# Two decoder blocks on one core: factors shared by two engines, a mask and a norm in other places of VectorE's order, transposes by halves, and the end of a convolution one chunk sooner

## The reference

```python
h = rms_norm(x, norm_mix)
proj = h @ w_in            # sb q,k,v | gla q,k,v | g_out | g_low | two gates
log_a = log_sigmoid(g_low @ w_gate_up + b_gate_up) / 16
o_gla = gla_chunked(g_q, g_k, g_v, log_a)      # 4 heads, key width 128, value width 256
o_gla = rms_norm(o_gla, gla_norm) * silu(g_out)
mix = sigmoid(gate_sb) * (o_sb @ w_proj_sb) + sigmoid(gate_gla) * (o_gla @ w_proj_gla)
x = x + mix @ w_out
x = x + square(relu(rms_norm(x, norm_mlp) @ w_ff1)) @ w_ff2
x = rms_norm(x, norm_final)
...
xn = rms_norm_2(x, norm_mix_2)
proj = xn @ w_in_2         # nsa q, kv, gates | conv a, ag | mem q | three merge gates
kvm = rms_norm_2(mem, norm_mem) @ w_mem_kv     # its second half is vm
u = a * sigmoid(ag)
u = conv_general_dilated(pad(u), conv_w, 31 taps, depthwise) + conv_b
u = silu(layer_norm(u, conv_ln_g, conv_ln_b))
br_conv = u @ w_conv_out
merged = gm[0] * br_nsa + gm[1] * br_conv + gm[2] * br_mem
h = x + merged @ w_out
out = h + (silu(hn @ w_gate) * (hn @ w_up)) @ w_down    # hn = rms_norm_2(h, norm_ffn)
```

## Time and profile before

| | |
|---|---|
| median of 3 runs | 941.41 us (940.28 to 945.93) |
| profiled execution, its time | 946.68 us |
| profiled execution, its span | 944.9 us |
| mean granted TensorE clock over the span | 0.992 |
| TensorE matmul busy | 918.0 us (97%) |
| VectorE busy | 623.9 us (66%) |
| ScalarE busy | 518.3 us (55%) |
| GpSimd busy | 93.1 us (10%) |

### The profile page before, as it was taken

The page is one execution under the profiler, slowest core; times in us unless marked ns, Lnnn a source line. Parts: engine busy times, 40 slices in busy tenths (PEclk is TensorE's granted clock), DMA queues, the critical chain, the costliest instruction groups (busy, mean ns, idle before and its releaser), DMA issues.

```text
span 944.9 us, 14354 instructions
## 1 busy us (share of the span) xinstructions
PE 918.0 (97%) x5800; PEld 813.2 (86%) x5800; DVE 623.9 (66%) x773; ACT 518.3 (55%) x728; POOL 93.1 (10%) x200
## 2 busy tenths in 40 slices
PE   8998999999999999999999999999998999999998
PEld 7996778899989888888879988889997788888887
DVE  5533565877766655566685888878967576566564
ACT  6544675665546444444466778876354555444451
POOL 8503343231010000000000000000000000000000
PEclk9998999999999999999999999999999999999999
DMA  8654242447555555555564852444435455655551
GB/s 270 201 179 133 92 131 89 135 147 251 173 180 179 174 198 205 181 178 178 181 179 132 266 179 90 135 134 126 138 98 176 133 179 183 205 185 182 178 178 45
DMA packets 115673, 155.36 MB, mean 164 GB/s; under 512 B 2649, under 2 KB 94913, under 8 KB 115618
## 3 DMA queue, kind: packets, MB, share of 16 engines
q1 hardware_dynamic: 114704, 151.57, 49.3%
q0 software_dynamic: 864, 2.98, 0.9%
q10 hardware_dynamic: 50, 0.04, 0.0%
HBM read 153.53 MB, written 1.05 MB: 164 GB/s over the span
## 4 chain that ended last, share of the span: by engine, by line
PE 80%; DVE 7%; ACT 7%; issue 3%; POOL 2%; DMA 1%; SPq 0%; ACTq 0%; DVEq 0%; POOLq 0%
PE PS L604 16%; PE PS L606 16%; PE PS L605 16%; PE PS L929 15%; PE PS L931 8%; DVE wlo L1791 3%; ACT whi L1232 2%; POOL TMP L224 2%; PE PS L831 1%; PE PS L1062 1%; PE PS L1040 1%; ACT TMP L1600 1%; PE PS L974 1%; DMA res<-in_x_dram 1%; DVE hT L1875 1%
## 5 line engine op out<-in xcount | busy, mean ns | idle before, releaser
L1791 DVE TENSOR_TENSOR wlo<-raw,whi 128x2048 fp32r<-128x2048 f32 x140 | 322.1, 2301 | 165.1 <-ACT whi L1232 165.0
L1232 ACT CAST whi<-raw 128x2048 fp32r<-128x2048 f32 x141 | 268.7, 1906 | 124.0 <-PE PS L606 124.0
L929 PE MATMUL PS<-hT,whi 128*128 128x512 f32 x608 | 216.9, 400 | 1.5 <-DVE hT L1875 1.5
L604 PE MATMUL PS<-hT,whi 128*128 128x256 f32 (+1 forms) x616 | 177.1, 288 | 2.3 <-DVE hT L1875 2.1
L605 PE MATMUL PS<-hT,whi 128*128 128x256 f32 (+1 forms) x616 | 174.2, 283 | 0.0
L606 PE MATMUL PS<-hT,wlo 128*128 128x256 f32 (+1 forms) x616 | 174.2, 283 | 0.0
L931 PE MATMUL PS<-hT,wlo 128*128 128x256 f32 x608 | 171.0, 281 | 0.0
L929 PEld LDWEIGHTS PS<-hT,whi 128*128 128x128 f32 x608 | 114.9, 189 | 30.1 <-issue 1.7
L604 PEld LDWEIGHTS PS<-hT,whi 128*128 128x128 f32 (+1 forms) x616 | 117.5, 191 | 4.0 <-issue 2.7
L605 PEld LDWEIGHTS PS<-hT,whi 128*128 128x128 f32 (+1 forms) x616 | 117.5, 191 | 0.2
L606 PEld LDWEIGHTS PS<-hT,wlo 128*128 128x128 f32 (+1 forms) x616 | 117.5, 191 | 0.0
(11 more groups left out here) (360 smaller groups left out, 1287.0 us busy)
## 6 DMA issues: line engine op xcount, KB each, us to landing
raw<-in_w_in_dram SPq DMA_DIRECT2D x47, 1024.0 KB, 5.2
raw<-in_w_ff_dram SPq DMA_DIRECT2D x32, 1024.0 KB, 5.2
raw<-in_w_gate_dram SPq DMA_DIRECT2D x11, 1024.0 KB, 5.3
raw<-in_w_up_dram SPq DMA_DIRECT2D x11, 1024.0 KB, 5.3
raw<-in_w_down_dram SPq DMA_DIRECT2D x11, 1024.0 KB, 5.0
raw<-in_w_out_dram SPq DMA_DIRECT2D x8, 1024.0 KB, 4.9
raw<-in_w_proj_gla_dram SPq DMA_DIRECT2D x4, 1024.0 KB, 5.0
raw<-in_w_mem_kv_dram SPq DMA_DIRECT2D x4, 1024.0 KB, 5.1
```

Source lines behind the costliest of these rows:

```text
L604: pe.matmul(dst, a_hi, b_hi, start=start, stop=False, skip_group_check=True)
L929: pe.matmul(PS[:, bank + c, :], w_hi[:, k, f], hT[:, k, :, :].rearrange("p w t -> p (w t)"), start=k == 0, stop=False, skip_group_check=True)
L1232: act.copy(whi[:, n % RING, :], raw[:, n % RING, :]).then_inc(hi_made, 1)
L1791: dve.tensor_tensor(wlo[:, n % RING, :], raw[:, n % RING, :], whi[:, n % RING, :].bitcast(F32), ALU.subtract).then_inc(lo_made, 1)
```

## The change

Five edits. (1) Units 0 and 1 are shared between GpSimd and VectorE as units 5 to 7 are (`SHARED_UNITS`, `upper_factors`, at chunks 9 and 11). (2) The norm of head 0 moves on VectorE from behind the mask of chunk 14 to a place ahead of the split of chunk 17. (3) At chunk 18 the mask of unit 4 moves on VectorE from behind the split of chunk 21 to a place between the banks of gout2 and gout3; its reduce stays. (4) VectorE scales x in four half pieces, first both first halves, and TensorE turns the first two pairs half a token block sooner in vm1, the other two where it turned all. (5) The last steps of the convolution move from s = 29 to s = 28, VectorE's product ahead of the split and ScalarE's rounding behind it; seven taps move from late and middle places to others.

```diff
-        LATE_UNITS, LOW_LEVELS = (5, 6, 7), 4
+        SHARED_UNITS, LOW_LEVELS = (0, 1, 5, 6, 7), 4
...
-                for l in range(LOW_LEVELS if u in LATE_UNITS else LEVELS):
+                for l in range(LOW_LEVELS if u in SHARED_UNITS else LEVELS):
                     ins = gla_factor(pool, u, l)
...
-                        if between and (a, k) == (1, 2):
-                            between()
+                        if between and a == 1 and k % 2 == 0:
+                            between(k // 2)
...
-                pe.wait_ge(xn_made, XN_BEFORE[event] + 3)
+                pe.wait_ge(xn_made, XN_BEFORE[event] + (3 if event == 2 else 2 * (pairs[-1] // 2) + 2))
...
-            half_of_pair("vm1", oT_hi, oT_lo, between=lambda: turn_normed(3, range(4)))
+            half_of_pair("vm1", oT_hi, oT_lo, between=lambda i: turn_normed(3, (2 * i, 2 * i + 1)))
...
-                if s == 29:
+                split_hi(n + RING)
+                if s == 28:
                     act.wait_ge(cv_f, 1)
                     act.activation(oT_hi[:, 4:8, :], u_flat.rearrange("p (f t) -> p f t", f=4), ACT.Copy,
                                    scale=0.5).then_inc(cv_hi, 1)
-                split_hi(n + RING)
...
+            def upper_factors(u):
+
+                dve.wait_ge(gf_exp, u + 1)
+                if u >= 1:
+                    dve.wait_ge(gs_made, u)
+                for l in range(LOW_LEVELS, LEVELS):
+                    gla_factor(dve, u, l)
+                gla_carry(dve, u).then_inc(gf_up, 1)
...
                     for half in (list(at)[n - 1], name):
+                        if (n, half) == (18, name):
+                            gla_mask(4)
                         evac(half)
                         evac_end(half)
+                    if n == 14:
+                        gla_norm(0)
...
+                if n in (9, 11):
+                    upper_factors((n - 9) // 2)
...
                 if 0 <= n - 10 < 16 and (n - 10) % 2 == 0:
-                    gla_mask((n - 10) // 2)
+                    if n != 18:
+                        gla_mask((n - 10) // 2)
+                    gla_reduce((n - 10) // 2)
...
-                if n in (14, 17, 21, 25):
+                if n in (17, 21, 25):
                     gla_norm((n - 13) // 4)
...
-            dve.tensor_scalar(xn[:, 0, :], res[:, 0, :], stat[:, 5, 4:5], None, ALU.mult).then_inc(xn_made, 1)
             for half in range(2):
-                scaled_half(5, res, 1, half)
+                for a in range(TT):
+                    scaled_half(5, res, a, half)
...
-            TAPS_AT = [0, 0, 0, 0, 2, 2, 2, 0, 1, 0, 4, 5, 8, 6, 6, 8, 8, 8, 8, 8, 8, 9, 9, 8, 7, 7]
+            TAPS_AT = [0, 0, 0, 0, 2, 2, 2, 0, 1, 0, 6, 5, 8, 6, 6, 8, 8, 8, 8, 11, 8, 9, 8, 7, 6, 5]
...
-                if s == 29:
+                if s == 28:
                     dve.wait_ge(cv_sig, 1)
                     dve.scalar_tensor_tensor(u_flat, u_flat, 1.0, cacc_flat, ALU.add, ALU.mult).then_inc(cv_f, 1)
...
-                if s == 29:
+                if s == 28:
                     dve.wait_ge(cv_hi, 1)
                     dve.scalar_tensor_tensor(oT_lo[:, 4:8, :], u_flat.rearrange("p (f t) -> p f t", f=4), 0.5,
                                              oT_hi[:, 4:8, :].bitcast(F32), ALU.mult, ALU.subtract).then_inc(cv_lo, 1)
```

More of the change, by code:

```diff
@@ L421, in two_block_kernel @@
         ROOTS_BEFORE = {0: 0, 1: 1, 2: 2, 3: 4, 5: 6, 4: 7}
-        XN_BEFORE = {0: 0, 1: 3, 2: 5, 3: 8, 4: 11}
+        XN_BEFORE = {0: 0, 1: 3, 2: 5, 3: 8, 4: 12}
         LAST_OF = {2: at["wout3"], 3: after_ffn1 - 1, 4: FFN2 - 1}
@@ L544, in gla_factors @@
                     pool.wait_ge(gs_made, u)
-                for l in range(LOW_LEVELS if u in LATE_UNITS else LEVELS):
+                for l in range(LOW_LEVELS if u in SHARED_UNITS else LEVELS):
                     ins = gla_factor(pool, u, l)
-                if u in LATE_UNITS:
+                if u in SHARED_UNITS:
                     ins.then_inc(gf_qk, 1)
@@ L824, in gla_scores @@
                 pe.wait_ge(gf_qk, u + 1)
-                if u in LATE_UNITS:
-                    pe.wait_ge(gf_up, LATE_UNITS.index(u) + 1)
+                if u in SHARED_UNITS:
+                    pe.wait_ge(gf_up, SHARED_UNITS.index(u) + 1)
                 for l in range(LEVELS):
@@ L1913, in gla_gate @@
                 dve.tensor_tensor(a_lo[a], t, a_hi[a].bitcast(F32), ALU.subtract).then_inc(ga_made, 1)
+            def upper_factors(u):
[5 more added lines that the diff above has]
+                gla_carry(dve, u).then_inc(gf_up, 1)
             def gla_mask(u):
-                h, a = u // 2, u % 2
                 dve.wait_ge(gs_made, u + 1)
@@ L1919, in gla_mask, with gla_reduce @@
                                   mask.rearrange("p l t -> p (l t)"), ALU.mult).then_inc(gs_masked, 1)
+            def gla_reduce(u):
+                h, a = u // 2, u % 2
                 if h >= 1:
@@ L1971, in _ @@
                 if n in (19, 21, 23):
-                    dve.wait_ge(gf_exp, (n - 9) // 2 + 1)
-                    for l in range(LOW_LEVELS, LEVELS):
-                        gla_factor(dve, (n - 9) // 2, l)
-                    gla_carry(dve, (n - 9) // 2).then_inc(gf_up, 1)
+                    upper_factors((n - 9) // 2)
                 split_lo(n + RING)
```

## The result

The changed kernel takes 930.57 us (median of 4, 930.24 to 933.54) against 943.50 us of the kernel before (median of 4, 940.28 to 945.93). The ratio is 0.9868, interval 0.9837 to 0.9899, so the change is faster by 1.0 to 1.6%. The profiled execution took 933.54 us with a span of 931.8 and a mean clock of 0.996, so against the profiled one of before (946.68) it gained 13.1. The other three had spans of 928.5 to 929.0 at 0.998 to 1.00.

What follows compares the result with a forecast made beforehand. TensorE was taken to bound the kernel, busy nearly the whole span, with its waits and clock falls the time to win. Terms 7.4 + 0.8 + 0.5 - 0.1 + 6.3 = 14.9 us, off the 941.4 median: 926.5 us, range 921.5 to 933.

Steps and rivals of the forecast that it cites:

- Part 1: Factors of units 0 and 1: 3.4 us wait, 3.4 clock fall and 0.56 at unit 1 go; 7.4 us gained.
- Part 2: Head 0's norm: TensorE's 1.10 us wait goes, unit 3's scores wait about 0.3 more; 0.8 us gained.
- Part 3: Mask of unit 4: unit 5's sums lose their 1.6 us wait, its scores then wait 1.5; 0.5 us gained.
- rival 4: Clock falls where it now holds, at vm1 and the chunk behind; one fall gives 929.9 us, five 943.5; chance 0.03.
- Part 4: x turned by halves around vm1: waits only move, VectorE's queue ends slightly later; -0.1 us.
- Part 5: Convolution's end: 3.8 us wait at ogc0, 1.7 of clock behind it and 0.8 of taps go; 6.3 us gained.
- the drain of ogc0's bank at ogc1: Sign of being wrong: new waits at ogc1, where VectorE is free only some 0.2 us before TensorE needs it.
- the 5.1 us of clock: Clock falls behind the waits at unit 0's scores (3.4 us) and ogc0 (1.7 us), expected to go with those waits.
- rival 1: Waits go but the clock falls all the same behind small products; gain 9.8 us, 931.6 us; chance 0.12.
- Rival 2: GpSimd and VectorE hold each other out at units 0 and 1; gain 12.9, 928.5 us; chance 0.10.
- Rival 3: The mask's move keeps all it removes, unit 5's factors coming earlier: 1.6 + 0.45 for 0.5, 924.9 us; chance 0.07.

Runs made afterwards that it cites:

- the filler in the kernel before: Kernel before with 28 unused small matmuls on TensorE ahead of its 3.42 us wait for unit 0's factors; median 943.18 us against 946.27, ratio 0.997.
- part 3 alone: Kernel before with only the mask of unit 4 moved ahead of gout3's bank; median 945.54 us over 12 executions, ratio 0.9993.

## Why the prediction was nearly right, and where it was wrong

**The mechanisms and the waits.** 926.5 us was forecast, 930.57 came; the gain was 14.9 by the sum, 13.1 between the profiled executions and 12.9 between the medians. Of the 4.1 us between forecast and result, 2.0 are missing gain; the other 2.1 come from the median of before, which stood at 941.41 when I subtracted and at 943.50 in the comparison. The waits, without the clock, were 9.8 us of the sum (14.9 less 3.4 and 1.7). Before, the profiled execution lost 3.4 and 1.7 us to two falls and 0.4 to the one near 755, so without them its span would be 939.4; three executions of the changed kernel had 928.5 to 929.0. That is 10.4 to 10.9, of which 0.4 is the earlier start. So the waits were sized well, and the clock wasn't.

**Part 1** was right: 6.9 for unit 0 where the sum had 6.8, and 0.8 for unit 1 where it had 0.56. GpSimd's eight products ended at 78.6, where I had put them at 79.3, since the durations of 0.35 overlap when one follows the other.

**Part 2** gave 0.77 (forecast 0.8). The wait at unit 3 grew by 0.56 where I had 0.3.

**Part 3** moved the wait as I worked out, from 1.6 at the sums to 1.83 at the scores (forecast 1.5), and kept 0.55 (forecast 0.5). What I missed stands in my own list: I wrote that the two falls stood behind waits of over 3 us and that "the waits of 1.1 and 1.6 us have none near them", and took from this that a wait of 1.5 has no fall. The same trace had a third fall, behind a wait of 1.50, which I did not look for: the mean clock of 0.992 stood for 945 x 0.008 = 7.6 us, and I had found 5.1. With 1.83 us it had one in three profiled executions of the changed kernel out of three, of 3.1, 1.5 and 1.6 us. I had the mechanism as rival 4, at vm1, where the wait is 1.3 us and the clock held. In the profiled execution this one term is more than the whole difference to the sum; the start, the tail, unit 1 and the small gains between make up the rest.

**Part 4** cost 0.13 (forecast 0.1). **Part 5** gave 5.6 for the end (forecast 5.5) and 0.7 for the taps (0.8); the drain of ogc0's bank at ogc1, for which I saw 0.2 us of room, brought no wait.

**The step that failed** besides this is the sentence "I subtract from the median because all terms are waits on chip that every execution has". The waits are; the 5.1 us of clock aren't. The profiled execution of before, at a mean clock of 0.992, was one of the worst; the medians beside the experiments stood at 0.996, 0.995 and 0.993, so that 3.8, 4.7 and 6.6 us of work were lost to the clock in all, where the profile lost 7.6 by the same reckoning (945 x 0.008). The changed kernel lost 2.8 on the two chips on which I ran it again (median 0.997). So the clock gave back 1.0 us and 3.8 us there, each to about 1 us (a mean clock is given to 0.001), not 5.1. One more sign: the profiled execution of before took 946.68, 5.3 above the median that I subtracted from, and 946.7 - 14.9 = 931.8 would have fitted, for the profiled execution of after took 933.54, and 3.1 less without its fall. Even the executions of the changed kernel at a clock of 1.00 took 930.2 to 930.5, so the forecast of 926.5 was out of reach without any new fall.

**The number against the rivals.** 930.57 lies nearer to the sums of rival 1 (931.6) and of rival 4 with one fall (929.9) than to 926.5, though rival 1's mechanism is refuted and rival 4's fall came at another place. It lies in the stated range because that was wide enough to hold them, not because the clock's terms were right. The chance of 0.88 for faster was also added up wrongly: the four terms named give 0.91.

**Rival 1** (the clock falls all the same) is refuted at both places by the windows after, and at unit 0 by the filler in the kernel before too. **Rival 2** (the engines hold each other out): at unit 0 GpSimd's products took 344 ns each at the median and started every 0.305 us, against 0.29 alone, so 0.12 us over eight of them. At unit 5 it does happen: the eighth product stood beside a split and took 2365 ns.

```profile
L224 POOL TENSOR_TENSOR TMP<-TMP,AR x8: 316/344/368, 76.2 to 78.3; 128x64 f32<-128x64 f32 x8
L224 DVE TENSOR_TENSOR TMP<-TMP,AR x6: 226/380/387, 76.1 to 77.5; 128x64 f32<-128x64 f32 x6
...
L224 POOL TENSOR_TENSOR TMP<-TMP,AR x8: 323/358/2365, 162.5 to 164.7; 128x64 f32<-128x64 f32 x8
```

These are minimum, median and maximum in ns, for unit 0 on both engines and for unit 5 on GpSimd. The Trainium skill, in SBUF — State Buffer, "SBUF: two separate sides", says that the first of the two engines to start keeps the port pair for its whole instruction; the eighth product agrees. The short ones don't show it: an estimate from the rows is 8 x 0.29 + 6 x 0.226 = 3.7 us if each had held the other engine out for its whole length, and GpSimd was done in 2.44. For a shared unit this says that short products run beside each other at little cost, and that no long instruction of the other engine should start before the last of them. **Rival 3** is refuted by the wait of 1.83 and the gain of 0.55.

**Open** is what decides whether a given wait is followed by a fall, and how long that is. The same 1.83 us had 3.1, 1.5 and 1.6 us in the changed kernel and none with part 3 alone; unit 0's 3.4 us had 3.4 in two traces and 1.7 in one; the 1.50 us ahead of the second feed-forward part had a fall in five traces of fourteen, while the 1.65 us at unit 5's sums had none in the five traces that have that wait. The Trainium skill, in TensorE: Matmul & The Clock Gate, "What's actually happening", says that the hardware looks at TensorE's activity over stretches that run on by themselves and don't begin with the kernel. That would give such a spread behind the same wait; no run here shows the stretches themselves.

## What to carry to other kernels

A wait that is moved is not only late by what is left of it: if it gets longer than those of its kind before, it can take the clock with it, and a gain of 0.5 us turns into a loss of 1 to 2.6. Before you move one, look at what it joins; after, compare two equal instructions on both sides of it, since their length shows the clock at once.

A term of the clock is no term of a wait. Read it from several executions (one less the mean clock, times span), not from the profiled one, and read it as an upper bound: where TensorE would soon have waited for another engine, a fall of 1.7 us of work cost 0.4. Compare it with the falls that you have found, to see if one is missing. Then take the wait itself into the median in full and the clock with the share that the executions show. Where a wait can't be removed, filler products in it keep the clock up, but count their time: 14 of them fit into 1.83 us and 28 cost 1.1.

Where two engines share short products, keep the long instruction of either one behind the last product of the other, and move what TensorE needs next ahead of that long one as well.

## What the runs showed of the hardware

A wait of 1.83 us was enough for TensorE's clock to fall from 2.4 to 1.2 GHz behind it, for 1.5 to 3.1 us of work, and one of 1.82 at the same place of another kernel was not. In the three profiled executions of the changed kernel the 14 products right behind the wait took 1.77, 2.11 and 2.92 us (1.77 at unit 3, where the clock held): in one of them the clock fell only after these products, in two inside them. Fifteen falls stand in the fourteen traces, each behind a wait of about 1.5 us or more; by the windows twelve cost 1.7 us of full-speed work and three 3.4, and the length of the wait doesn't sort them (3.4 us at unit 0 had both, 1.83 at unit 5 too).

28 products that nobody reads, put into a wait of 3.42 us, made the kernel before 3.1 us faster.

The eighth of eight short products of GpSimd took 2365 ns beside a split of VectorE of 2.4 us, where the eight have a minimum of 323 and a median of 358 ns beside VectorE's short products. The split itself was hardly longer (2.40 in place of 2.29).
